# Expert stage of a mixture-of-experts layer: four buffers of gathered rows and four of output rows, gathers issued two blocks ahead

## The reference

```python
def routed_experts(h, idx, w, w_e1, w_e3, w_e2):
    ...
    # 640 tokens x 8 experts each; sorted by expert, padded to blocks of 128 rows
    xd = jnp.zeros((n_rows, d), h.dtype).at[dest].set(h[stok])
    ...
    def run_block(args):
        xb, e = args
        return swiglu(xb, w_e1[e], w_e3[e], w_e2[e])     # (silu(x @ w1) * (x @ w3)) @ w2

    yd = lax.map(run_block, (xd.reshape(n_blocks, EXPERT_BLOCK, d), blk_e)).reshape(n_rows, d)
    return jax.ops.segment_sum(yd * wd[:, None], td, num_segments=t)
```

## Time and profile before

| what | value |
|---|---|
| median of 3 runs | 1845.75 us (1842.26 to 1846.2) |
| the profiled execution, its own time | 1849.71 us |
| its span, first to last instruction | 1847.9 us |
| mean granted TensorE clock | 0.956 |
| busy share of PE, DVE, ACT, POOL | 89%, 50%, 39%, 32% |
| moved by DMA | 352.01 MB, mean 190 GB/s |
| blocks in the expert stage | 70 |

### The profile page before, as it was taken

The page is one execution under the profiler, slowest core; times in us unless marked ns, Lnnn a source line. Parts: engine busy times, 40 slices in busy tenths (PEclk is TensorE's granted clock), DMA queues, the critical chain, the costliest instruction groups (busy, mean ns, idle before and its releaser), DMA issues. The chain is left out here.

```text
span 1847.9 us, 22495 instructions
## 1 busy us (share of the span) xinstructions
PE 1641.5 (89%) x7863; PEld 1195.4 (65%) x7863; DVE 922.0 (50%) x1341; ACT 722.0 (39%) x1054; POOL 597.6 (32%) x675
## 2 busy tenths in 40 slices
PE   7798999869999899999987599999999999999991
PEld 2587665557787799995553366666666666666660
DVE  2956454455666401111562366555565555655653
ACT  3432232222333312210210356566655566655650
POOL 0542100031110333330007245444444444444440
PEclk9999899988999999999988799999999999999995
DMA  8310323100000423225243499999999999999944
GB/s 312 123 54 1 132 98 107 66 0 1 1 1 24 137 68 87 73 68 200 73 191 128 160 339 364 367 349 340 340 351 352 337 345 340 339 334 337 343 163 173
DMA packets 121162, 352.01 MB, mean 190 GB/s; under 512 B 21162, under 2 KB 60670, under 8 KB 94088
## 3 DMA queue, kind: packets, MB, share of 16 engines
q1 hardware_dynamic: 89434, 237.25, 35.0%
q10 hardware_dynamic: 10224, 71.83, 10.5%
q0 software_dynamic: 21440, 42.08, 9.1%
HBM read 334.66 MB, written 47.87 MB: 207 GB/s over the span
## 5 line engine op out<-in xcount | busy, mean ns | idle before, releaser
L2088 DVE TENSOR_TENSOR e_wlo<-mem,e_whi 128x2048 fp32r<-128x2048 f32 x140 | 314.6, 2289 | 105.2 <-ACT e_whi L2028 105.2
L2028 ACT ACTIVATE e_whi<-mem 128x2048 fp32r<-128x2048 f32 x140 | 260.3, 1909 | 24.1 <-DMA mem<-in_w_e 14.5
L1998 PE MATMUL psum<-mem 128*128 128x512 f32 x560 | 252.0, 593 | 1.5 <-ACT mem L2060 1.5
L1978 PE MATMUL psum<-e_whi,e_xhi 128*128 128x512 f32 x560 | 228.1, 407 | 7.1 <-DVE e_xlo L2095 7.1
L1980 PE MATMUL psum<-e_wlo,e_xhi 128*128 128x512 f32 x560 | 222.1, 397 | 0.0
L1979 PE MATMUL psum<-e_whi,e_xlo 128*128 128x512 f32 x560 | 221.9, 396 | 0.0
L1935 POOL TENSOR_TENSOR held<-nhalf 1x1 f32<-1x1 f32 x206 | 125.2, 608 | 285.4 <-DMA sums<-mem_h,si 115.6
L1998 PEld LDWEIGHTS psum<-mem 128*128 128x128 f32 x560 | 101.0, 190 | 102.2 <-issue 102.1
L908 ACT ACTIVATE mem<-psum,small 128x640 f32<-128x640 f32 (+1 forms) x80 | 56.8, 710 | 217.7 <-DVE small L1026 217.7
L2095 DVE TENSOR_TENSOR e_xlo<-psum,e_xhi 128x512 fp32r<-128x512 f32 x140 | 90.2, 686 | 78.0 <-ACT e_xhi L2034 78.0
L1978 PEld LDWEIGHTS psum<-e_whi,e_xhi 128*128 128x128 f32 x560 | 105.7, 189 | 30.1 <-DVE e_xlo L2095 7.8
(11 more groups left out here) (287 smaller groups left out, 3253.4 us busy)
## 6 DMA issues: line engine op xcount, KB each, us to landing
mem<-in_w_e SPq DMA_DIRECT2D x144, 1024.0 KB, 12.6
mem<-in_w_e ACTq DMA_DIRECT2D x66, 1024.0 KB, 11.0
mem<-in_w_mod SPq DMA_DIRECT2D x24, 1024.0 KB, 5.2
mem<-in_w_in SPq DMA_DIRECT2D x3, 2048.0 KB, 8.9
sums<-mem SPq DMA_DIRECT2D x10, 512.0 KB
mem<-sums SPq DMA_DIRECT2D x10, 512.0 KB, 7.9
mem<-in_x_sample SPq DMA_DIRECT2D x8, 512.0 KB, 11.2
wkvb<-in_w_in SPq DMA_DIRECT2D x8, 512.0 KB, 4.5
```

The lines of the kernel that those rows point to most:

```text
L1978: pe.matmul(out, xh, wh, start=first, stop=False)
L1998: mm = pe.matmul(pY[:, cs], gT[:, f, :], w2[v][:, f, cs], start=(f == 0), stop=(f == 1))
L2028: act.activation(wHi13[u % 2][:, a], w13[u][:, a], ACT.Copy).then_inc(se["h13"], 1)
L2088: dve.tensor_tensor(wLo13[u][:, a], w13[u][:, a], wHi13[u % 2][:, a].bitcast(F32), ALU.subtract)\
```

## The change

The rows fetched for a block go to one of four buffers in place of two, and so do the output rows; the new buffers lie in memory that earlier stages used. The gather that stands in POOL's step n is now the one for block n+2 and waits for the transposes of block n-2. The gathers for blocks 2 and 3 wait instead for two memsets of the new buffers on DVE (`s_xz`), which themselves wait until the shared expert's output, which lay there, has been stored (`s_acc`). ACT's output copy of block m waits for the scatter of block m-4 rather than m-2. The waits of `scatter` itself are not touched, nor is the table's own wait on the sums.

```diff
--- before.py
+++ after.py
@@ -1408,7 +1408,7 @@
     triX, triI = cst[0:NE, 385:449], cst[0:NE, 449:513]
     recs = mem.at(M_SC + 8192, NT * TOPK, 4).bitcast(I32)
     kidx = mem.at(M_SC + 8352, NT * TOPK).bitcast(I32)
-    tabs = mem.at(M_TB + 9288, NBLK + RING + 1, 4).bitcast(I32)
+    tabs = mem.at(M_TB + 9288, NBLK + RING + 2, 4).bitcast(I32)
 
     w13 = [mem.at(M_R + 6144 * ((u + 1) % RING), 2, KT, FE) for u in range(RING)]
     w2 = [mem.at(M_R + 6144 * ((u + 1) % RING) + 4096, 2, D) for u in range(RING)]
@@ -1656,8 +1656,8 @@
     def load_w2(sp, n, u):
         sp.dma_start(w2[u], w2_src[:, bass.ds(n, 1)].rearrange("p e f n -> p (e f) n")).then_inc(s_w2[u], 16)
 
-    xg = [mem.at(B0 + 768 + 1024 * b, D) for b in range(2)]
-    yb = [mem.at(M_H + 4096, D), mem.at(B0 + 2816, D)]
+    xg = [mem.at(o, D) for o in (B0 + 768, B0 + 1792, M_OB + 1024, M_OB + 2048)]
+    yb = [mem.at(o, D) for o in (M_H + 4096, B0 + 2816, M_OB + 3072, M_OB + 4096)]
 
 
     def halves(name, byte, *shape):
@@ -1669,11 +1669,12 @@
     wLo13 = [halves(f"e_wlo13_{u}", ring_at[u], 2, KT, FE) for u in range(RING)]
     xHi, xLo = halves("e_xhi", wkvb_at, KT, P), halves("e_xlo", wkvb_at + 4 * 1024, KT, P)
     held = sb("held", [1, 2])
-    gi = [sb(f"gi{b}", [P, 1], I32) for b in range(2)]
+    gi = [sb(f"gi{b}", [P, 1], I32) for b in range(4)]
     si = [sb(f"si{b}", [P, 1], I32) for b in range(2)]
     names = ("gi", "si", "Tx", "xh", "xl", "h13", "l13", "u", "sl", "g", "Th", "te", "y", "ye", "z")
     se = {n: sem(f"s_e_{n}") for n in names}
-    s_xg = [sem(f"s_xg{b}") for b in range(2)]
+    s_xg = [sem(f"s_xg{b}") for b in range(4)]
+    s_xz = sem("s_xz")
     s_zero = sem("s_zero")
     s_acc0 = sem("s_acc0")
     s_sc = [sem(f"s_sc{b}") for b in range(2)]
@@ -1938,12 +1939,13 @@
                 first = isinstance(n, int)
 
                 def gather():
-                    if first and n == 0:
-                        return
-                    b = (u + 1) % 2
-                    pool.wait_ge(se["Tx"], n)
-                    pool.tensor_copy(gi[b][:, :], wslot(tabs, n + 1, 0)).then_inc(se["gi"], 1)
-                    pool.wait_ge(se["gi"], n + 2)
+                    b = (u + 2) % 4
+                    if first and n < 2:
+                        pool.wait_ge(s_xz, n + 1)
+                    else:
+                        pool.wait_ge(se["Tx"], n - 1)
+                    pool.tensor_copy(gi[b][:, :], wslot(tabs, n + 2, 0)).then_inc(se["gi"], 1)
+                    pool.wait_ge(se["gi"], n + 3)
                     hold(pool)
                     pool.indirect_dma_start(out=xg[b], out_offset=None, in_=S["h2"],
                                             in_offset=bass.IndirectOffsetOnAxis(ap=gi[b][:, 0:1], axis=0),
@@ -1960,10 +1962,10 @@
                     hold(pool)
 
                     pool.indirect_dma_start(out=sums[b], out_offset=bass.IndirectOffsetOnAxis(ap=si[b][:, 0:1], axis=0),
-                                            in_=yb[b], in_offset=None, compute_op=ALU.add,
+                                            in_=yb[(u - 3) % 4], in_offset=None, compute_op=ALU.add,
                                             bounds_check=TOK - 1, oob_is_err=False).then_inc(s_sc[b], 16)
 
-                due(pool, guard(-1), gather)
+                due(pool, guard(-2), gather)
                 due(pool, guard(3), scatter)
 
             nb = run(pool, step)
@@ -1981,9 +1983,9 @@
 
             def step(n, i, u, guard):
                 def turn_x():
-                    pe.wait_ge(s_xg[u % 2], 32 * i + 16 * (u // 2 + 1))
+                    pe.wait_ge(s_xg[u], 16 * (i + 1))
                     for k in range(KT):
-                        tr = pe.transpose(pX[:, k * P:(k + 1) * P], xg[u % 2][:, k * P:(k + 1) * P], ident[:, :])
+                        tr = pe.transpose(pX[:, k * P:(k + 1) * P], xg[u][:, k * P:(k + 1) * P], ident[:, :])
                     tr.then_inc(se["Tx"], 1)
 
                 def down():
@@ -2042,9 +2044,9 @@
                 def take_y():
                     m = n - 2
                     act.wait_ge(se["y"], m + 1)
-                    if not (isinstance(n, int) and m < 2):
-                        act.wait_ge(s_sc[u % 2], 32 * i + 16 * ((u - 2) // 2))
-                    act.activation(yb[u % 2], pY, ACT.Copy, scale=wslot(tabs, m, 2).bitcast(F32)).then_inc(se["ye"], 1)
+                    if not (isinstance(n, int) and m < 4):
+                        act.wait_ge(s_sc[u % 2], 32 * i + 16 * ((u - 2) // 2) - 16)
+                    act.activation(yb[(u - 2) % 4], pY, ACT.Copy, scale=wslot(tabs, m, 2).bitcast(F32)).then_inc(se["ye"], 1)
 
                 def next_w2():
                     if guard(-2) is None:
@@ -2110,6 +2112,9 @@
                 due(dve, guard(-1), next_w13)
                 due(dve, guard(0), product)
 
+            dve.wait_ge(s_acc, 16 * NT)
+            for b in (2, 3):
+                dve.memset(xg[b], 0.0).then_inc(s_xz, 1)
             lo_w13(0, 0)
             run(dve, step)
```

## The result

The change makes the kernel slower: a median of 1854.06 us in 8 runs (1850.23 to 1856.79) beside 1845.97 us for the kernel before (8 runs, 1842.26 to 1849.36), a ratio of 1.0043 with a 95% interval of 1.0029 to 1.0058. The forecast was 1842.0 us, in a range to 1850, so both the sign and the range are wrong. The profiled execution took 1853.5 us (span 1851.7) where before it took 1849.7 (span 1847.9). These two single executions lie 3.8 us apart and the medians 8.1; the stages ahead, which the change does not touch, end at 1035.6 us here and at 1041.8 us in the profile of before (first load of the first block's transposes). That start differs by as much between kernels whose earlier stages are the same: over all fourteen traces of this case it lies between 1032.0 and 1041.8 us. The expert stage itself is therefore the thing to compare, and it is done here block by block.

A forecast was written before the change was run, and what follows sets the result against it. The prediction took the DMA engines to bound the kernel from about 1156 us, at 11.03 us a block. Its terms, -4.0 + 0.8 - 0.6 = -3.8 us, took the median from 1845.75 to 1842.0 us, range 1827 to 1850.

The forecast's parts named there:

- paragraph on the rule: DMA engines take queues in turn, so early gathers take turns from weights; interleaved rows would load half the engines; no size.
- Term (1): Expert blocks: gathers issued a block earlier let PE run further ahead until the weights are late; gain 4.0 us once.
- (2): DMA queues: one gather more takes DMA time ahead of the late weights; cost 0.8 us.
- (3): From 1700 to 1790 us: PE's short waits there are covered by a gather's reserve; gain 0.6 us.
- Term (4): ACT's output copy: four buffers remove its scatter waits, which lie in spare time; worth 0, 0.8 us kept for the range.
- Term (5): Start: two memsets of 0.912 us ahead of DVE's first low half are hidden; under 1.8 us if not.
- A: Expert blocks: the DMA engines have a reserve and the 0.88 us a block goes, giving 1801 us; 4 in 100.
- B: Expert blocks: part of the loss goes as the DMA's idle 2% becomes work, giving 1831 us; 11 in 100.
- C: End of stage: scatters left over drain after the last block, +10.8 us, giving 1852.8 us; 9 in 100.
- D: POOL's order ties a gather to a scatter, so gather waits stay and time is 1845.75 us; 4 in 100.
- list of signs: Gather waits nearly gone, weight waits grow, PE waits for ACT or DVE, first stall four or five blocks later, period 10.9 to 11.1.

The follow-up runs named there:

- early gathers alone: Kernel after with the output side put back: four row buffers, gathers two blocks ahead, two output buffers and ACT's old wait; 1847.69 us, ratio 1.0011.
- outputs moved: Kernel before with its two output buffers put in the memory the change uses for its new ones; 1844.57 us, ratio 0.9998.
- output half: Kernel before with four output buffers and ACT's later wait, its gathers and two row buffers as they were; 1850.14 us, ratio 1.0035.
- rows spread: Kernel before, table read back so a block's real rows spread evenly over the DMA engines; 1804.18 us, ratio 0.9777. On the kernel after: 1803.09 us, 0.9771.

## Why the prediction was wrong

**What bounds the kernel.** Right as far as it went: DMA-bound from 1156 us on, PE's pace 10.15 us, and a gather asked for earlier would only uncover the weights. But "the period, 11.03 us, is what the DMA engines need for a block's bytes" was taken from a mean share of 0.98. The same bytes pass in 10.14 us when the rows are spread. The prediction also reads landing times that grow "for all queues at once". Its rows are those of the scatter alone, which doubled from 9.1 to 19.7 us, while the median for the w2 loads went from 9.2 us (1066 to 1086 us) to 11.1 (1200 to 1700 us). The prediction names the uneven load of the engines in its paragraph on the rule and then lets it change nothing, neither the sum nor a rival.

**Term (1), gathers a block earlier, 4.0 us once.** The mechanism held to the letter: no gather waits, stall moved behind the transposes, pace of PE kept for 14 blocks, -3.4 us in the change and -3.8 us in the gathers alone. What failed is the word "gain". It is a loan: PE runs ahead of the weights by that much and gives it back at the end, where it waits for the last weights, and these come no sooner. The last half of w13 lands 740.8 us behind the first transposes in the early gathers alone (1772.9 - 1032.1), and 740.8 us behind them in "outputs moved" (1777.2 - 1036.4), whose gathers are those of before. **Terms (2) and (3)** are where it was given back. An extra gather in the queue was put at 0.8 us on the ground that a plain read must be cheaper than a scatter that adds, which no row shows; blocks 16 to 60 took 1.5 us more, which is within the scatter of that span, so the traces neither confirm nor refute the 0.8. The last blocks were put at a gain of 0.6 and were a loss of 2.4, which is a wrong sign. The three together give 1847.69 us measured, where the forecast had 1842.0.

**Term (4), four output buffers worth 0: the step that failed.** The waits on ACT were in spare time, as said, and lifting them brought nothing. The sentence that costs the rest, "The w2 load behind that copy on ACT's queue moves up by as much; it lands in 11 us and is wanted more than two blocks later", asks only whether the moved load is late. It had to put a price on the place at which the load enters among the others when the engines are full. "By as much" was too little as well: the waits on ACT are 1.2 us each (34.7 / 28), and in the output half the issue moved by 3.1 us, from 5.3 to 2.2 (medians). The output half costs 1.0035, some 6.5 us, and 1.0001 once the load is held back; the load alone, moved early in the kernel before, costs 1.0024. The output half is so about half of the miss of 12.1 us (1854.06 against 1842.0); the rest is terms (1) to (3). The old wait had been pacing that load by accident. From whom the early load takes turns was not shown.

**Term (5), the start.** Right. DVE's two memsets stand at 1035.84 and 1036.91 us, and PE's first up matmul comes 1043.42 - 1035.57 = 7.85 us behind the first transposes, where before it came 7.76 us behind them (1049.54 - 1041.78):

```profile
1035.57 1.57 PEld L1988 LDWEIGHTS psum<-ident,mem 128*128 128x128 f32 x8 [26.29 <-issue]
1035.84 0.91 DVE L2117 MEMSET mem<- 128x1024 f32 x1 [33.33 <-PEq L1689]
1043.42 0.80 PE L1980 MATMUL psum<-e_whi,e_xhi 128*128 128x512 f32 x1 [5.88 <-DVE e_xlo L2097]
```

**The rivals.** A's time, 1801 us, is nearly what the rows spread give, 1804, but it needed capacity that this change does not free. B did not occur: the period rose from 11.04 to 11.22 us and the share went from 0.98 to 0.97, not up. C named 1852.8 us and the result is 1854, yet by another road. At the end of the stage POOL waits for ACT's output by the same two amounts as in the earlier trace rows, and no scatters are bunched:

```profile
1807.86 0.18 POOL L1936 TENSOR_TENSOR held<-nhalf 1x1 f32<-1x1 f32 x1 [6.72 <-ACT mem_h L2049]
1813.26 0.18 POOL L1936 TENSOR_TENSOR held<-nhalf 1x1 f32<-1x1 f32 x1 [2.84 <-ACT mem L2049]
```

D is refuted by the gather waits, which are gone. The slower side was given 14 in 100, on one mechanism; the release of a transfer into full engines, which the prediction itself describes, was not among the rivals. What was right, and not by luck, is the list of signs: the gather waits are gone, the weight waits grew, PE waits before the down matmuls, and the first block over 10.2 us comes four blocks later. Two of them failed: the period (11.22 us, for 10.9 to 11.1) and the rate (339 GB/s, for some 343).

## What to carry to other kernels

With the DMA engines full, the deeper prefetch here only lent time to the ramp and took it back at the end; and a wait that is removed also releases the DMA issues queued behind it, so list those and ask of each what its new place costs, even when nobody is waiting for it; that price was found here by moving the load alone. Before that, ask whether the engines are full evenly, for instance by the times of a load's sixteen increments: a mean share of 0.98 hid a layout of rows that cost 2.2% of the run, and a few lines that spread them gained ten times what was forecast for the prefetch. The version to keep is the kernel before with its rows spread, 1804.18 us against 1845.55.

## What was unexpected of the hardware

- A copy of 128 int32 on POOL takes 178 ns, and 2247 ns where it begins beside DVE's long instruction, whose 4.49 us for two make 2.25 each. In the block shown above it starts at 1406.70 us, where the first of DVE's two should end (1404.41 + 2.25), and ends with the second, so it seems to wait for it. It cost nothing here.
- A DMA issue on ACT's queue is not tied to the ACTIVATEs written ahead of it: in the kernel after it goes out at 1402.85 us, while the output copy that stands before it in the program starts at 1406.10 us. What had held it before was the wait, not its place in the order.
- The time of issue of one 1 MB load a block, with much slack, moved the total by 0.24% when 2.7 us earlier and by 0.83% when 3.1 us later (medians of the steady stretch).
- Under uneven load each w2 load of 1 MB lands in two groups of eight parts, 4.43 us apart; with the rows of the gathers and scatters spread, the gap is 0.06 us.
- The DMA share does not tell how full the engines are: 0.98 at 343 GB/s, 1.02 at 372 GB/s. A mean share above 1 means that the times of packets on one engine overlap.
